# First mixer: the last eight modulation blocks are weighted on VectorE instead of TensorE, and the gate products sit among the filter spectra

## The reference, cut to what matters

```python
mod_x = jnp.split((jax.nn.silu(c) @ w_ada[l] + b_ada[l])[:, None, :], N_MOD, axis=-1)
mod_c = jnp.split((jax.nn.silu(c_ctx) @ w_ada[l] + b_ada[l])[None, None, :], N_MOD, axis=-1)
```

## Time and profile before

| | |
|---|---|
| median of three runs | 1598.09 us |
| profiled execution | 1596.44 us, span 1594.6 us |
| PE busy | 1324.2 us (83%) |
| VectorE busy | 468.3 us (29%) |
| ScalarE busy | 295.9 us (19%) |
| mean granted TensorE clock | 0.928 of full speed |

### The profile page before, as it was taken

The page is one execution under the profiler, slowest core; times in us unless marked ns, Lnnn a source line. Parts: engine busy times, 40 slices in busy tenths (PEclk is TensorE's granted clock), DMA queues, the critical chain, the costliest instruction groups (busy, mean ns, idle before and its releaser), DMA issues. The chain is left out here.

```text
span 1594.6 us, 18796 instructions
## 1 busy us (share of the span) xinstructions
PE 1324.2 (83%) x7712; PEld 750.1 (47%) x7712; DVE 468.3 (29%) x1108; ACT 295.9 (19%) x616; POOL 0.2 (0%) x4
## 2 busy tenths in 40 slices
PE   6999999956755656599999999766999989998558
PEld 4665877412311212177667743322576677443213
DVE  5225563101101101014663522210236644321102
ACT  2422212100000000022322312200223223122002
POOL 0000000000000000000000000000000000000000
PEclk9999999977778878899999999977999999999879
DMA  9475388999999999992421499999915214899994
GB/s 392 168 260 211 132 344 326 429 427 427 427 428 428 428 428 427 428 425 102 186 106 53 167 394 384 419 424 421 390 53 211 98 61 159 345 380 421 423 421 200
DMA packets 39390, 492.50 MB, mean 309 GB/s; under 512 B 4352, under 2 KB 4736, under 8 KB 5888
## 3 DMA queue, kind: packets, MB, share of 16 engines
q1 hardware_dynamic: 39152, 491.06, 74.6%
q10 hardware_dynamic: 144, 0.13, 0.0%
HBM read 490.13 MB, written 1.05 MB: 308 GB/s over the span
## 5 line engine op out<-in xcount | busy, mean ns | idle before, releaser
L659 PE MATMUL PS<-A 128*128 128x256 f32 (+4 forms) x1552 | 365.1, 393 | 5.5 <-DMA A<-ring_d 1.8
L1023 PE MATMUL PS<-A 128*32 128x512 f32 x1472 | 220.9, 738 | 133.0 <-DMA A<-ring_d 133.0
L659 PEld LDWEIGHTS PS<-A 128*128 128x128 f32 x1552 | 273.4, 194 | 89.1 <-issue 51.2
L1023 PEld LDWEIGHTS PS<-A 128*32 128x32 f32 x1472 | 50.0, 123 | 292.0 <-issue 230.6
L1613 PE MATMUL PS<-A 128*32 128x512 f32 (+1 forms) x768 | 114.2, 680 | 76.7 <-DMA A<-ranked_d 76.7
L1613 PEld LDWEIGHTS PS<-A 128*32 128x32 f32 (+1 forms) x768 | 32.7, 128 | 148.2 <-issue 148.2
L2167 DVE TENSOR_TENSOR A<-A,PS 128x512 f32<-128x512 f32 x8 | 5.5, 687 | 315.1 <-PE PS L1023 315.1
L1640 PE MATMUL PS<-A 128*32 128x512 f32 (+1 forms) x512 | 80.3, 597 | 0.3 <-issue 0.3
L2678 DVE TENSOR_TENSOR A<-A,PS 128x256 f32<-128x256 f32 x22 | 9.3, 421 | 232.1 <-ACT A L3233 232.1
L664 PE MATMUL PS<-A 128*128 128x128 f32 (+1 forms) x396 | 59.1, 281 | 18.3 <-DVE A L2167 7.1
L664 PEld LDWEIGHTS PS<-A 128*128 128x128 f32 (+1 forms) x396 | 45.2, 145 | 56.1 <-issue 30.9
(11 more groups left out here) (405 smaller groups left out, 1301.0 us busy)
## 6 DMA issues: line engine op xcount, KB each, us to landing
A<-ring_d SPq DMA_DIRECT2D x155, 2048.0 KB, 25.5
A<-ranked_d SPq DMA_DIRECT2D x48, 2048.0 KB, 11.9
A<-ranked_d SPq DMA_DIRECT2D x48, 1024.0 KB, 19.2
A<-ring_d SPq DMA_DIRECT2D x2, 1312.0 KB, 28.1
A<-ring_d SPq DMA_DIRECT2D x2, 1280.0 KB, 23.9
A<-p_d SPq DMA_DIRECT2D x1, 1152.0 KB, 31.2
A<-xT_d SPq DMA_DIRECT2D x1, 1024.0 KB, 5.3
A<-cT_d SPq DMA_DIRECT2D x1, 1024.0 KB, 11.7
```

Source lines behind the costliest of these rows:

```text
L659: ins = g.matmul(out, l, r, start=n == 0, stop=n == len(pairs) - 1)
L1023: ins = g.matmul(ps[32 * e:32 * e + 32, :], rows_of(kk, e), wv[4 * (kk % 2) + e], start=kk == 0, stop=kk == 7)
```

## The change

Blocks 4 to 11 are cut in halves of four chunks. VectorE multiplies each chunk with its per-partition scalar of silu(c) and adds it to an accumulator of 128 x 512 per block (`ACC`, which lies where `SPEC` will be). A new step `asum` on TensorE sums the eight accumulators over their partitions with a column of ones (`STRIP`), 8 matmuls into the bank that `ada` filled before; the bank is no longer held from block 4 on. Blocks 5, 7, 9 and 11 use slot 11, which stood empty in the mixer, and the others share the three old slots. VectorE's part of `sp` waits for `asum`, as it overwrites `ACC`. `g 2` and `g 3` move from the projections to the filters, ahead of `sp 0` and of `sp 1`. The core of the diff:

```diff
-COST = dict(ada=4, hy=8, ...
+COST = dict(ada=0.75, asum=4, hy=8, ...
-         ("mod", 1): ("ic", 0, 3), ("sp", 0): ("ada", 9), ("sp", 1): ("ada", 10)}
+         ("mod", 1): ("ic", 0, 3), ("sp", 0): ("asum",)}
-FILTERS = [...] + [("sp", 0), ("sp", 1)]
+FILTERS = [...] + [("g", 2), ("sp", 0), ("g", 3), ("sp", 1)]
-    + [("g", j) for j in range(4)]
+    + [("g", j) for j in range(2)]
-LATE = [("ada", b) for b in range(4, 12)] + [("mod", 1)]
+LATE = [("ada", b, half) for b in range(4, 12) for half in range(2)] + [("asum",), ("mod", 1)]
...
+ODD_ADA = [("ada", b) for b in range(5, 12, 2)]      # these go to LAST_SLOT in mixer_slots
...
             def ada(blk, half=None):                  # TensorE
+                if half == 0:
+                    ada_blocks[blk] = weights("ada", blk)
+                if half is not None:
+                    return
...
+            def asum():
+                ps = fresh("ada", 1)
+                g.wait_ge(*at("strip"))
+                for blk in range(4, 12):
+                    q, c = blk % 4, 14 - 2 * (blk - 4)
+                    g.wait_ge(*at("acc", blk))
+                    ins = g.matmul(ps[32 * q:32 * q + 32, :], STRIP[:, c:c + 32], ACC[:, blk - 4, :], start=blk < 8, stop=blk >= 8, skip_group_check=True)
+                ins.then_inc(*full("ada", 1))
...
+            def ada(blk, half=None):                  # VectorE
+                if half is None:
+                    return
+                w, i = ada_blocks[blk]
+                wv, acc = w.rearrange("p (k n) -> p k n", k=8), ACC[:, blk - 4, :]
+                v.wait_ge(*at("scp"))
+                v.wait_ge(*at("landed", i))
+                for k in range(4 * half, 4 * half + 4):
+                    if k == 0:
+                        ins = v.tensor_scalar(acc, wv[:, k, :], SCP[:, k, 14:15], None, ALU.mult)
+                    else:
+                        settle()
+                        ins = v.scalar_tensor_tensor(out=acc, in0=wv[:, k, :], scalar=SCP[:, k, 14:15], in1=acc, op0=ALU.mult, op1=ALU.add)
+                    ins.then_inc(*(out("acc", blk) if k == 7 else out()))
+                if half:
+                    note("dve", "read", i)
             def sp(o):                                # VectorE
+                v.wait_ge(*at("full", "ada", 1))
```

More of the change, by code:

```diff
@@ L114, in ranks @@
     return range(4, 8) if j == 2 else range(2 * j, 2 * j + 2)
-COST = dict(ada=4, hy=8, ht=2, sp=8, ut=2, cv=8, ic=2, q=8, k=8, v=16, g=8, csum=8, xsum=8, a=12, b=20, kt=14, st=20, qk=16, scr=4, o=8, osum=10,
+COST = dict(ada=0.75, asum=4, hy=8, ht=2, sp=8, ut=2, cv=8, ic=2, q=8, k=8, v=16, g=8, csum=8, xsum=8, a=12, b=20, kt=14, st=20, qk=16, scr=4, o=8, osum=10,
             kx=8, cq=16, ckv=8, cqsum=2, kvsum=1, kpe=2, vm=2, qa=4, km=2, qb=2, ca=16, cb=2, kir=2, vc=13, bkr=1, ix=1, tk=2,
@@ L163 @@
          ("mod", 0), ("hm", 1), ("hm", 0), ("hz",)]
-FILTERS = [("ht", odd, od) for odd in range(2) for od in range(4)] + [("sp", 0), ("sp", 1)]
+FILTERS = [("ht", odd, od) for odd in range(2) for od in range(4)] + [("g", 2), ("sp", 0), ("g", 3), ("sp", 1)]
 CONV = [("hy", m) for m in range(4)] + [("ut", 0, 0), ("ut", 0, 1), ("cv", 0)] + [("hy", m) for m in range(4, 8)] \
@@ L242 @@
 YE_SLOT, HM_SLOT, XS_SLOT, T_SLOT, LAST_SLOT, HID_SLOT = 7, 8, 9, 10, 11, 12
+ODD_ADA = [("ada", b) for b in range(5, 12, 2)]
 def mixer_slots():
-    use = {}
+    use, beside, order = {}, [], []
     for n, (kind, *a) in enumerate(MIX1):
@@ L250, in mixer_slots @@
                    hy=lambda: ("hy", a[0] // 4), out=lambda: ("out", a[0] // 2)).get(kind, lambda: None)()
-        if key:
+        if key and key not in ODD_ADA:
             use[key] = (use.get(key, (n, n))[0], n)
+        elif key and key not in beside:
+            beside.append(key)
+            order.append((n, LAST_SLOT))
     through, slots = [-1] * NM, []
@@ L257, in mixer_slots @@
         through[x] = last
-        slots.append(x)
+        slots.append((first, x))
     in_order = sorted(range(NM), key=lambda x: through[x])
-    return [in_order.index(x) for x in slots]
+    return [x for n, x in sorted([(n, in_order.index(x)) for n, x in slots] + order)]
 FIRST_BLOCKS = [0, 11, 10, 3, 1, 2, 4, 9, 5, 6, 7, 8]
@@ L465, in program @@
         E1, K1, KT = [[take(2, 256), CH[:, 2 * x:2 * x + 2, :]] for x in range(3)]
+        STRIP = take(46)
+        assert mem.top <= COLS - SLOT
+        ACC = SPEC.rearrange("p o x a c -> p (o x a) c")
         aF = T[:, 2:4, :]
@@ L632, in branch_ring @@
             return RING[SLOTS[N_MIX + 96 + 58 * l + BRANCH_BLOCK]]
+        ada_blocks = {}
         def tensor(g):
@@ L716, in sp @@
                         ins.then_inc(*full("sp", o, x))
-            def ada(blk):
-                n = int(blk > 3)
-                first, last = ((0, 3), (4, 11))[n]
+            def ada(blk, half=None):
[3 more added lines that the diff above has]
+                    return
+                n, first, last = 0, 0, 3
                 w, i = weights("ada", blk)
@@ L989, in tensor @@
             sig.stage = "mix"
-            steps = dict(w1=w1, w2=w2, ht=ht, sp=sp, ada=ada, mod=mod, xsum=xsum, csum=csum, hy=hy, ut=ut, cv=cv, ic=ic,
+            steps = dict(w1=w1, w2=w2, ht=ht, sp=sp, ada=ada, asum=asum, mod=mod, xsum=xsum, csum=csum, hy=hy, ut=ut, cv=cv, ic=ic,
                          q=q, k=k, v=v, g=gate, a=a_, gates=gates, b=b, kt=kt, st=st, scr=scr, o=o_, osum=osum, ob=ob, wr=wr, out=out_, rows=rows)
@@ L1806, in vector @@
             v.memset(SCP, 0.0).then_inc(*out("scp0"))
+            v.memset(STRIP, 0.0).then_inc(*out())
+            settle()
+            v.memset(STRIP[:, 14:15], 1.0).then_inc(*out("strip"))
             def w1():
@@ L2035, in rows @@
                 ins.then_inc(*out("bn1", b))
-            steps = dict(w1=w1, w2=w2, hz=hz_, ht=ht, sp=sp, mod=mod, xsq=xsq, xs=xs, hm=modulate, csq=csq, cs=cs, hy=hy, cv=cv, ic=ic,
+            steps = dict(w1=w1, w2=w2, hz=hz_, ht=ht, sp=sp, ada=ada, mod=mod, xsq=xsq, xs=xs, hm=modulate, csq=csq, cs=cs, hy=hy, cv=cv, ic=ic,
                          a=a_, gates=gates, b=b, st=st, qk=qk, scr=scr, osum=osum, ob=ob, wr=wr, out=out_, rows=rows)
@@ L2827, in cv, with ada, ada_row @@
                 odd_times("cv", o)
[L2829 to L2832, removed]
+            def ada(blk, half=None):
+                if blk == 3:
+                    ada_row(0)
+            def ada_row(n):
                 full("ada", n)
@@ L2950, in rows @@
                 s.activation(HT[:, :, b * 256:(b + 1) * 256], bank("htt", b).rearrange("p (t c) -> p t c", t=2), ACT.Copy).then_inc(*out("htt", b))
-            steps = dict(w2=lambda: sine(0), hz=lambda: sine(1), sp=sp, ada=ada, xsq=xsq, xsum=xsum, hm=modulate, csq=csq, csum=csum,
+            steps = dict(w2=lambda: sine(0), hz=lambda: sine(1), sp=sp, ada=ada, asum=lambda: ada_row(1), xsq=xsq, xsum=xsum, hm=modulate, csq=csq, csum=csum,
                          hy=hy, ut=ut, cv=cv, q=q, k=k, v=vv, g=gate, gates=gates, b=b, kt=kt, qk=qk, o=o_, osum=osum, rows=rows)
```

## The result

The changed kernel takes 1616.38 us (median of 4 runs, 1612.02 to 1621.11) against 1597.47 us before: ratio 1.0118, 95% interval 1.009 to 1.0145. The forecast was 1614 us, slower, with 1601 to 1621 as its range. The profiled execution took 1612.02 us, span 1610.2 us.

A forecast was written before the change was run, and what follows sets the result against it. PE was taken to bound the mixer. A 13.0 us shift at cv 0 plus 3.8 us of clock loss gave 16.8 us on the profiled 1596.4, 1613.2; with the median 1.65 higher, 1614.9, stated as 1614, range 1601 to 1621.

The forecast's parts named there:

- PE saves 13.0 us: On PE in the mixer: eight late blocks, 14.8 us, are removed and asum adds 1.85 us, a gain of 13.0 us.
- DVE's queue sets `asum`: DVE's queue from block 4 at 70.8 us, with eight blocks of 45.7 us, lets asum start at 144.6; chance 55%.
- Waits of PE: PE waits 3.0 us in st 0 1, 8.4 at g 0, 1.5 for a bank and 11.1 at asum.
- Clock behind the two long waits, 3.8 us: Half clock after PE's waits at g 0 and asum adds 1.8 and 2.0 us.
- From `asum` to `cv 0`: PE's steps from asum's start to cv 0 take 39.0 us, including a 2.5 us wait ahead of o 0.
- The walk: Stepping through each engine's ordered list with estimated prices, plus 0.1 us a step; it put cv 0 at 183.6 us.
- `cv 0`: The mixer's cv 0 starts at 183.6 us instead of 170.6, +13.0 us before clock losses; 184 to 188 expected in the trace.
- The shift passes to the end: The later ring-bound stream can't absorb a shift: what cv 0 starts later, the kernel ends later.
- the prediction's own sign: Test stated beforehand: the forecast is wrong if cv 0 starts before 171 or its shift isn't the shift at the end.
- first rival: All of DVE's added work is hidden, so the 13.0 us gain comes through: 1585 us; chance 10%.
- third rival: Longer than walked: later ring blocks, 0.8 us instructions or half clock behind the 2.5 us waits; 1618 to 1624 us; chance 13%.
- Semaphores between VectorE instructions: In DVE's blocks: by the skill page waits are free, saving 6 us for about 1608; the forecast priced the gaps instead.

The follow-up runs named there:

- e11: Changed kernel with block g requested early, qk 1, scr 1 0 and scr 1 1 in their old places, half of VectorE's multiplications left out: 1590.88 us, ratio 0.9962.
- e9: The changed kernel run once more, unchanged, on another chip than its first follow-up runs: 1618.30 us, ratio 1.0132 against the kernel before.
- e3: Changed kernel with unread matmuls keeping PE busy in the two long waits, ahead of block g and at asum: 1609.60 us, ratio 1.0081.
- e8: Changed kernel with qk 1, scr 1 0 and scr 1 1 put back in their old places: 1605.75 us, ratio 1.0061.
- e10: Changed kernel with block g requested early, qk 1, scr 1 0 and scr 1 1 in their old places, 12 unread matmuls ahead of asum: 1604.02 us, ratio 1.0033.
- e12: Changed kernel with accumulators in slot 11, half blocks spread out, hy 0's block requested early, qk 1, scr 1 0, scr 1 1 in old places: 1595.15 us, ratio 0.998.
- e4: Changed kernel with blocks 4, 6, 8 and 10 back on TensorE, only 5, 7, 9 and 11 on VectorE: 1622.16 us, ratio 1.0163.
- e5: Changed kernel with accumulators in slot 11, all blocks in the three old slots, half blocks spread to about 195 us, asum after ic 0 1: 1611.06 us, ratio 1.0106.
- e2: Changed kernel with block g requested ahead of ada 8 in the order of DMAs: 1614.23 us, ratio 1.0115.

## Why the prediction was right, and which term was missing

- **PE saves 13.0 us.** Held up to `cv 0`: e11 has it 9.7 us earlier, with 3.3 us of waiting at `asum` in it.
- **DVE's queue sets `asum`.** Held, but 3 us earlier than forecast. With 1.8 us for the clock, 146.4 was predicted; the last pair starts at 143.41 in e9, and at 144.83 in the profile above, which came into the stretch 1.6 us late. Block 4 starts at 69.67 in e9 and not at 70.8, and from there to the last half block it takes 73.7 us and not 75.6. The blocks take more than priced: an instruction starts 0.80 us after the last, not 0.73, and the first of a block takes 0.48 us, not 0.57 (48.0 us for eight blocks, not 45.7; and 0.752 us each, outside the 0.69 to 0.74 that was to show the forecast right). DVE's waits take less, 7.0 us where 9.4 and the 1.8 for the clock were put down. (That DVE worked 5 to 11 of 20 us before was read a little high: from 60 to 80 us it was 3.4, from 100 to 120 it was 4.3.)
- **Waits of PE.** 3.0, 8.4, 1.5 and 11.1 us predicted, 2.5, 7.3, 0.6 and 7.9 measured. The order was right. At `asum` PE arrives at 133.62 in e9, as walked (133.5), and 9.8 us pass to the last pair; 7.9 of them are the wait, as 14 of the 16 records go ahead of it.
- **Clock behind the two long waits, 3.8 us.** Both dips are there; e3 gives 5 to 8 us for them. A third dip, behind the 2.5 us in `st 0 1`, was put at nothing: `st 0 1` takes 1.98 us for 1.10 and the step behind it 4.45 for 3.72 in e9, 1.6 us. It comes ahead of the wait for block g, which takes it up.
- **From `asum` to `cv 0`.** This is the term that was mis-sized. From the end of `asum`, 37.15 us and 2 for the clock were predicted, and 42.0 measured in e9. The walk had the wait of 2.5 us ahead of `o 0`, yet gave it no loss of clock, since rows of such a loss were at hand only for long waits. e9 against e8: 6 us of half clock, 3 of them ahead of `cv 0` and 3 in it.
- **`cv 0`.** 183.6 and 3.8 for the clock make 187.4; e9 has 187.32. That this is so close is luck: `asum` came 3 us early and the clock behind `o 0` took 3 us. The other 3 us are in `cv 0` itself and stay.
- **The shift passes to the end.** Held through the experts and, to a few us, to the end. These are the experts' matmuls before and after: shortest, median and longest in ns, then first and last start in us.

```profile
L1023 PE MATMUL PS<-A x1472: 588/593/1063, 274.4 to 676.6; 128*32 128x512 f32 x184
L1047 PE MATMUL PS<-A x1472: 589/593/1063, 293.5 to 695.7; 128*32 128x512 f32 x184
```

  Both take 402.2 us, so this stretch, in which PE waits for the ring, passes on a shift of 19.1 us in full (e9: 292.2 to 694.6). Behind it the executions differ whatever the kernel: to the end of the span it takes 918.0 us before, 914.5 changed, 921.0 in e9, 918.2 in e8, 917.9 in e10, 920.0 in e11 and 914.9 in e12. So the profiled span of changed is 15.6 us longer than before and that of e9 21.0, for a shift of the experts that is the same to within 1.3 us. By the prediction's own sign (the shift at `cv 0` is the shift at the end) it is 18.0 us against 15.6 in changed and 16.5 against 21.0 in e9. The cause of this spread isn't shown.
- **Total.** 1614 was forecast, and 1616.4 and 1618.3 measured. The 6 us of half clock behind `o 0` that the forecast lacked are half hidden by `asum` coming 3 us early. The first rival (all hidden) needed less than 0.67 us an instruction and fell on that. Of the third rival two conditions came true, 0.8 us an instruction and half clock behind a wait of 2.5 us; its time, 1618 to 1624, was met by e9 (1618.3) and not by the first runs of changed.
- **Semaphores between VectorE instructions.** By the Trainium skill, "VectorE: DVE Perf Modes", section "The DRAIN you can't avoid", a wait between them is free, and the time would have been 1608. The changed trace sides with the rows: with a wait each instruction takes 0.752 us and leaves a gap of 0.05, where the ten independent ones overlap by 0.08. The same section also says that a next instruction that isn't held starts earlier, which is what those ten do. No run has the new form without its waits, so what they cost there isn't shown.

## What to carry to other kernels

That an engine is a quarter to a half busy doesn't say that work moved to it is free, when its queue is in step with that of the bottleneck: count what stands ahead of each eviction that PE waits for, and how long each ring slot is then held. A block that PE read in 1.9 us was held for 6 us and more by VectorE, and in the changed kernel, e4 and e5 this came out as a wait of 7 to 13 us for whatever block was next in the ring. Asking for the block that is needed first (e12) takes it away; where VectorE's queue is full (e2) the wait comes back as one for VectorE. After such a move, look at each new wait for the clock behind it, not only at its length: here one of 2.47 us cost 6 us more.

## What the runs showed of the hardware that was not expected

- A scalar_tensor_tensor of 128x512 with both tensors in SBUF and the second the output of the last one takes 752 ns and starts 0.80 us after it; the form with one tensor in PSUM takes 689 ns.
- Behind one wait of 2.47 us, in work of small matmuls, the granted clock stayed at 0.50 from about 181 to 195 us, with PE busy 7.2 of the 8 us from 184 to 192. The wait of 7.3 us ahead of `g 0` cost less: `g 0` took 5.5 us for 3.6, and at 118 us the clock was at 1.00. Without the 2.47 us (e8), the same steps ran at 1.00.
- The same length of wait can cost very different amounts. The 2.5 us in `st 0 1` cost 1.6 us of clock, the 2.47 us ahead of `o 0` 6 us. Behind the wait of 1.26 us at 49.5 us, which all kernels here have, the clock fell in some executions (changed, e3) and not in others (before, e9), for 1.6 and some 3 us.
- Two executions of kernels that are the same behind 700 us differ there by up to 6.5 us (914.5 changed, 921.0 e9). The changed kernel took 1612 to 1621 us in its first four runs and 1616 to 1619 in the four of e9. Its mean granted clock was 0.920 in the fastest run and 0.910 in the slowest. That the clock is the cause of the spread is not shown.
